# Moving head turns, feeds of merged sums and a wait for the last head into neighbouring matmul blocks of a two-block transformer kernel

## What is computed

```python
proj = x @ w_in                                   # first block
q_dsa, c_kv, q_idx, k_idx, w_idx, q_m, k_m, v_m, ga, gb = split(proj)
merged = sigmoid(ga + b0) * (o_a @ w_o_dsa) + sigmoid(gb + b1) * (o_b @ w_o_moba)
y = merged @ w_out
...
y = (silu(g) * u) @ w_ffn_out                     # g, u = split(x @ w_ffn_in)
...
merged2 = sum(sigmoid(gate[n]) * (branch[n] @ w_up_2[n]) for n in range(3))
x = x + merged2 @ w_out_2                         # second block
```

## Time and profile before

| | |
|---|---|
| median of 3 runs | 2307.86 us (2304.59 to 2309.53) |
| the profiled execution | 2309.78 us, span 2307.9 us |
| PE, busy share of the span | 98% |
| DVE, ACT, POOL, busy share | 57%, 45%, 7% |
| mean granted clock of PE | 0.992 of full |
| moved by DMA | 421 MB, 182 GB/s on average |

### The profile page before, as it was taken

How to read it: one execution, slowest core, us unless ns; L and a number is a source line. 1 busy time by engine, 2 the same in 40 slices (tenths; PEclk the granted TensorE clock), 3 DMA queues, 4 the chain that set the end, 5 groups by cost and what they waited for, 6 DMA issues and landing times.

```text
span 2307.9 us, 30089 instructions
## 1 busy us (share of the span) xinstructions
PE 2253.7 (98%) x10189; PEld 1855.2 (80%) x10189; DVE 1305.9 (57%) x1571; ACT 1044.2 (45%) x1243; POOL 168.3 (7%) x175
## 2 busy tenths in 40 slices
PE   9999999999999899999999999998999999999999
PEld 7777888888877678878887888786888788888887
DVE  5445655666657665445444444457655566645664
ACT  4333444555434444433444344344445444545643
POOL 1000000001204040000000000004000000200020
PEclk9999999999999999999999999999999999999999
DMA  7654554655855456566665666554556565665555
GB/s 216 221 163 147 174 162 153 191 163 180 275 192 163 148 182 190 177 191 192 192 189 180 186 183 201 177 186 137 178 172 199 180 188 177 213 180 180 174 182 164
DMA packets 216698, 421.10 MB, mean 182 GB/s; under 512 B 15240, under 2 KB 19888, under 8 KB 214704
## 3 DMA queue, kind: packets, MB, share of 16 engines
q1 hardware_dynamic: 213456, 402.31, 56.6%
q0 software_dynamic: 3168, 17.82, 2.3%
HBM read 417.97 MB, written 2.11 MB: 182 GB/s over the span
## 4 chain that ended last, share of the span: by engine, by line
PE 94%; DVE 3%; ACT 1%; DMA 1%; issue 1%; DVEq 0%; SPq 0%; ACTq 0%
PE b_ps L543 88%; PE b_ps L585 1%; PE b_ps L568 1%; PE b_ps L628 1%; DVE b_w_lo L1321 1%; DVE b_x_res L1479 1%; PE b_ps L698 1%; DMA b_stage<-in_w_up 1%; DVE b_x_res L1470 1%; PE b_ps L643 1%; PE b_ps L637 0%; PE b_ps L716 0%; PE b_ps L644 0%; ACT b_nat L986 0%; DMA b_gate_a<-in_x 0%
## 5 line engine op out<-in xcount | busy, mean ns | idle before, releaser
L1321 DVE TENSOR_TENSOR b_w_lo<-b_stage,b_w_hi 128x1024 fp32r<-128x1024 f32 (+1 forms) x762 | 931.5, 1242 | 605.1 <-ACT b_w_hi L959 599.1
L959 ACT ACTIVATE b_w_hi<-b_stage 128x1024 fp32r<-128x1024 f32 (+1 forms) x762 | 793.9, 1054 | 706.2 <-PE b_ps L543 674.0
L543 PE MATMUL b_ps<-b_w_hi,b_x_hi 128*128 128x512 f32 (+1 forms) x2368 | 943.6, 399 | 4.5 <-DVE b_x_lo L1362 3.0
L543 PE MATMUL b_ps<-b_w_hi,b_x_lo 128*128 128x512 f32 (+1 forms) x2368 | 923.8, 390 | 0.0
L543 PE MATMUL b_ps<-b_w_lo,b_x_hi 128*128 128x512 f32 (+1 forms) x2368 | 922.5, 390 | 0.0
L543 PEld LDWEIGHTS b_ps<-b_w_hi,b_x_hi 128*128 128x128 f32 x2368 | 447.2, 189 | 101.1 <-issue 6.4
L543 PEld LDWEIGHTS b_ps<-b_w_hi,b_x_lo 128*128 128x128 f32 x2368 | 446.4, 189 | 94.1
L543 PEld LDWEIGHTS b_ps<-b_w_lo,b_x_hi 128*128 128x128 f32 x2368 | 447.3, 189 | 87.9
L543 PE MATMUL b_ps<-b_w_hi,b_ff_h 128*128 128x512 f32 x352 | 138.9, 395 | 6.2 <-DVE b_ff_l L1362 6.2
L543 PE MATMUL b_ps<-b_w_hi,b_ff_l 128*128 128x512 f32 x352 | 138.3, 393 | 0.0
L543 PE MATMUL b_ps<-b_w_lo,b_ff_h 128*128 128x512 f32 x352 | 138.2, 393 | 0.0
(11 more groups left out here) (280 smaller groups left out, 1463.0 us busy)
## 6 DMA issues: line engine op xcount, KB each, us to landing
b_stage<-in_w_in SPq DMA_DIRECT2D x336, 512.0 KB, 4.0
b_stage<-in_w_ffn_in SPq DMA_DIRECT2D x176, 512.0 KB, 4.5
b_stage<-in_w_ffn_out SPq DMA_DIRECT2D x88, 512.0 KB, 4.2
b_stage<-in_w_out SPq DMA_DIRECT2D x64, 512.0 KB, 4.3
b_stage<-in_w_up SPq DMA_DIRECT2D x24, 512.0 KB, 4.3
b_stage<-in_w_o_dsa SPq DMA_DIRECT2D x16, 512.0 KB, 4.3
b_stage<-in_w_o_moba SPq DMA_DIRECT2D x16, 512.0 KB, 4.3
b_stage<-in_w_kv_mem SPq DMA_DIRECT2D x16, 512.0 KB, 3.9
```

What stands on the lines that cost most here:

```text
L543: ins = mm(ps[:, ACC + r, 0:n], x[:, kt + t, rows], w[:, slot, t, 0:n], start=first and t == 0 and k == 0, stop=last and t == GK - 1 and k ...
L959: act.activation(w_hi[:, slot, :, 0:n], stage[:, slot, :, 0:n], ACT.Copy)\
L1321: dve.tensor_tensor(w_lo[:, slot, :, 0:n], stage[:, slot, :, 0:n], w_hi[:, slot, :, 0:n].bitcast(F32), ALU.subtract).then_inc(sem("lo_done ...
```

## The change

1. **Turns.** The 8 turns of the q and k projections stand behind group 0 of the block that follows, on PE and on DVE (which copies the heads there). The turn of the index keys and the latent (`keys_and_latent`, 7 transposes) stands behind group 2. The loops over these blocks are written out.
2. **Last turn of each `ffn_in` part.** It stands behind group 0 of the first `ffn_out` block, and that block waits for it only ahead of the group that reads its result.
3. **Last head.** The wait for `o_free` stands ahead of the last group of an up-projection block.
4. **Feeds of merged sums.** Batches of the feed stand behind groups of the up-projection blocks 1 to 3, as `FED_UP_B` and `FED_UP_2` say (block: {group: batch}), and the rest in the first block of the output projection. ACT and DVE have their parts at the same places.
5. **Bias table.** POOL waits for the end of the first branch's up-projection and for each of the 8 loads before it posts the next.
6. **Start.** The first weights are posted ahead of `x`; `keep_warm` runs 18 and 3 transposes in place of 12 and 10; ACT and DVE split the first group ahead of the first batch; DVE reads out the first block ahead of its last split.

```diff
+FED_UP_B = ({}, {2: 0, 3: 1}, {2: 2, 3: 3}, {2: 4, 3: 5}, {2: 6, 3: 7})
+FED_UP_2 = ({}, {1: 0}, {0: 1, 1: 2}, {0: 3, 1: 4}, {0: 5, 2: 6, 3: 7})
...
             x_chunk(0, 0, NB // 2)
-            group(a["w_in"], 0, C_LAT, FIRST_W)
             x_chunk(0, NB // 2, NB)
             group(a["w_in"], GK * P, C_LAT, FIRST_W)
...
+                    pool.wait_ge(sem("tile_out1"), c.at("ups0") + 4)
...
+                            pool.wait_ge(sem("rel"), c.next("rel", 16))
...
-            keep_warm(12)
-            feed_weights(x_in, x_landed, n=FIRST_W, warm=lambda: keep_warm(10))
-            with c.loop(pe, "q_idx", 2):
-                weights()
-                turn(left)
...
-            with c.loop(pe, "q_dsa", 2):
-                weights()
-                turn(left)
-            with c.loop(pe, "qk_m", 4):
-                pe.wait_ge(sem("qi_staged"), c.next("qi_staged"))
...
-                weights(hook=index_head)
-                turn(left)
-            for b in range(2):
-                weights()
+            keep_warm(18)
+            feed_weights(x_in, x_landed, n=FIRST_W, warm=lambda: keep_warm(3))
+            def turn_first(then=None):
+                def hook(j):
+                    if j == 0:
+                        turn(left)
+                    if then:
+                        then(j)
+                return hook
+            def keys_and_latent(j):
+                if j != 2:
...
+                T(ps[:, TP, S:S + P], kidx2[:, 0, :], ident[:, :]).then_inc(sem("tp_done"), 1)
...
+            def index_head(j):
...
+                if n == 0:
+                    pe.wait_ge(sem("qi_staged"), c.next("qi_staged"))
...
+            weights()
+            weights(hook=turn_first())
+            weights(hook=turn_first(keys_and_latent))
+            weights(hook=turn_first())
+            for b in range(4):
+                weights(hook=turn_first(index_head))
+            weights(hook=turn_first())
+            weights()
...
-            pe.wait_ge(sem("o_free"), c.value("o_free"))
+            def last_head_at(group_):
+                def before(j):
+                    if j == group_:
+                        pe.wait_ge(sem("o_free"), c.value("o_free"))
...
-                weights(kts=8, hi=oh, lo=ol)
+                weights(kts=8, hi=oh, lo=ol, before=last_head_at(3))
...
-            pe.wait_ge(sem("o_free"), c.value("o_free"))
-            with c.loop(pe, "up_b", 4):
-                weights(kts=8, hi=oh, lo=ol)
...
-            feed_weights(gate_a, merged_by("summed1"))
+            def feed_one(src, t):
+                pe.wait_ge(sem("tp_free"), c.value("tp_free", 0 if t == 0 else 1))
+                feed_batch(src, t)
+            def merged_by(mark, n):
+                pe.wait_ge(sem("summed"), max(1, c.at(mark) - D // NB + n + 1))
+            def feed_when(src, mark, batches):
+                def hook(j):
+                    if j in batches:
+                        t = batches[j]
+                        merged_by(mark, t // 2)
+                        feed_one(src, t)
+                return hook
+            def fed_by(j):
+                if j == 0:
+                    pe.wait_ge(sem("tp_free"), c.value("tp_free"))
+                elif j >= 5:
+                    pe.wait_ge(sem("tp_free"), c.value("tp_free", 7 - j))
+            for b in range(4):
+                weights(kts=8, hi=oh, lo=ol, before=last_head_at(3),
+                        hook=feed_when(gate_a, "summed1", FED_UP_B[b]))
+            weights(before=fed_by, hook=feed_when(gate_a, "summed1", FED_UP_B[4]))
...
-                turn(left)
-                pe.wait_ge(sem("tp_free"), c.value("tp_free"))
+                def last_tile_at(j):
+                    if j == 2 * (nf - 1):
+                        pe.wait_ge(sem("tp_free"), c.value("tp_free"))
+                weights(kts=4 * nf, hi=ff_h, lo=ff_l, before=last_tile_at, hook=turn_last)
...
-                pe.wait_ge(sem("o_free"), c.value("o_free"))
-                with c.loop(pe, f"up2_{n}", 2):
-                    for b in range(2):
-                        weights(kts=4, hi=y_h, lo=y_l)
-            feed_weights(merged2, merged_by("summed_b2"))
+                if n < 2:
+                    with c.loop(pe, f"up2_{n}", 2):
+                        for b in range(2):
+                            weights(kts=4, hi=y_h, lo=y_l, before=last_head_at(1))
+                else:
+                    for b in range(4):
+                        weights(kts=4, hi=y_h, lo=y_l, before=last_head_at(1),
+                                hook=feed_when(merged2, "summed_b2", FED_UP_2[b]))
+            weights(before=fed_by, hook=feed_when(merged2, "summed_b2", FED_UP_2[4]))
...
+            split()
             for t in range(KT // 2):
                 lo_batch(x_hi[:, 2 * t:2 * t + 2, :], x_lo[:, 2 * t:2 * t + 2, :], t)
-                split()
+                if t > 0:
+                    split()
                 c.next("w_used")
-            for _ in range(AHEAD):
-                split()
+            split()
             for r in range(R):
                 tile_done(r)
...
                 c.next(f"tile_out{r}")
...
+            def heads_of(b):
+                dst, b = (qi_t, b) if b < 2 else (qd_t, b - 2) if b < 4 else (qkm_t, b - 4)
+                heads_in(lambda t: dst[:, b * 4 + 2 * t:b * 4 + 2 * t + 2, :])
+            for b in range(8):
+                def q_hook(j):
+                    if b > 0 and j == 0:
+                        heads_of(b - 1)
+                        if b == 2:
+                            c.mark("q_idx", "tp_free")
+                    if b == 0:
+                        small_norms(j)
+                    if b == 2 and j == 2:
+                        keys_and_latent()
+                    if b >= 4:
+                        if j == 0 and b == 4:
...
             c.mark("ups_b", "tile_out1")
-            with c.loop(dve, "up_b", 4) as i:
-                weights(kts=8)
...
+            def feed_when(batches):
+                def hook(j):
+                    if j in batches:
+                        t = batches[j]
+                        lo_batch(x_hi[:, 2 * t:2 * t + 2, :], x_lo[:, 2 * t:2 * t + 2, :], t)
+                return hook
+            for b in range(4):
+                weights(kts=8, hook=feed_when(FED_UP_B[b]))
+                gated_at(gate_b, gate_a, slice(b * NB, (b + 1) * NB), True)
             c.mark("merged", "tile_out1")
-            feed_weights(x_hi, x_lo)
+            weights(hook=feed_when(FED_UP_B[4]))
             c.mark("fed", "tp_free")
...
-                product_lo(nf - 1)
                 alpha = ALPHA if f0 == 0 else 1.0
                 stat = f0 == FFN_PARTS[-1][0]
```

More of the change, by code:

```diff
@@ new lines, in index_head @@
+            def index_head(j):
+                if j % 2:
+                    return
+                n = j // 2
+                half = slice((n % 2) * IDX_D, (n % 2 + 1) * IDX_D)
+                if n == 0:
+                    pe.wait_ge(sem("qi_staged"), c.next("qi_staged"))
+                pe.wait_ge(sem("idx_read"), c.value("idx_read"))
+                for t, (lo, hi) in enumerate(TILE_COLS):
+                    ins = mm(ps[:, AUX, lo:hi], qi_st[half, n // 2, t * P:(t + 1) * P],
+                             kidx_t[half, 0:hi - lo], start=True, stop=True)
+                ins.then_inc(sem("idx_done"), 1)
+                c.next("idx_read")
@@ L1063, in _ @@
             c.next("tp_done", 2)
-            with c.loop(act, "q_dsa", 2):
+            for b in range(2):
                 weights()
@@ L1197, in _ @@
                     hidden(hook=lambda j: product_hi(i) if j == 0 else None)
-                product_hi(nf - 1)
+                weights(kts=4 * nf, hook=lambda j: product_hi(nf - 1) if j == 0 else None)
+                skip_block()
                 if nf == 4:
-                    with c.loop(act, f"ffn_out{f0}", 4):
+                    with c.loop(act, f"ffn_out{f0}", 3):
                         weights(kts=4 * nf)
@@ L1203, in _ @@
                 else:
-                    with c.loop(act, f"ffn_out{f0}", 2):
-                        for b in range(2):
-                            weights(kts=4 * nf)
-                            skip_block()
+                    for b in range(3):
+                        weights(kts=4 * nf)
+                        skip_block()
             root(sd[:, 0:R])
@@ L1579, in _ @@
             dve.wait_ge(sem("ext"), 32)
-            for b in range(2):
-                weights(hook=small_norms if b == 0 else None)
-                skip_block()
-                heads_in(lambda t: qi_t[:, b * 4 + 2 * t:b * 4 + 2 * t + 2, :])
-            c.mark("q_idx", "tp_free")
-            dve.wait_ge(sem("tp_done"), c.next("tp_done"))
-            dve.tensor_copy(kidx_t[:, :], ps[:, TP, 0:S]).then_inc(sem("tp_free"), 1)
-            dve.wait_ge(sem("tp_done"), c.next("tp_done"))
```

(31 more changed lines are left out.)

144 lines of the change are left out of this document (73 added, 71 removed).

## The result

The changed kernel takes 2311.46 us (median of 20 runs, 2308.12 to 2312.53) and the kernel before, run beside it, 2306.59 us (20 runs, 2303.46 to 2309.53): a ratio of 1.0018, 95% interval 1.0011 to 1.0024. It is 4.9 us slower, where 7.5 us less were forecast. The predicted time was 2300, its range 2292 to 2307.

What follows compares the result with a forecast made beforehand. PE was taken to bound the kernel (94% of the chain that ended last). Gains of 29.1 us against losses of 21.6 made -7.5, from 2309.78 to 2302.3, less 1.9 for the profiled execution: 2300, range 2292 to 2307.

Steps and rivals of the forecast that it cites:

- the turns of q and k: Between q and k projection blocks: turns moved behind a group 0 cost 0.79 us each; gain 6.5 us, bounds 5 to 7.
- the last turns of `ffn_in`: End of the three `ffn_in` parts: waits at the turn go, gain 8.7 us, plus 3.2 for two half-clock stretches.
- the last head: Before the first up-projection: PE's 1.4 us wait goes, as its first three groups read finished heads; gain 1.4 us.
- the bias table: First branch's up-projection: the late weight load's 3.4 us wait and 1.6 us half-clock stretch go; gain 5.0, bounds 0 to 5.0.
- the six new stalls: Up-projection block boundaries: `gated` queues behind `lo_batch` on DVE, so PE waits 2.3 us at each of six; loss 13.8 us.
- the feeds: Feeds of `merged` and `merged2`: 16 batches placed behind groups cost 7.7 us in place of 5.3 and 4.9; gain 2.6.
- the clock behind the stalls: After the six new stalls: half clock follows 3 of 6; loss 4.8 us, bounds 0 to 9.6.
- Loads behind the merge: At `w_out`: POOL's two load bursts become one, about one group of weights is missing; loss 3 us, bounds 0 to 11.
- The share of the weights: During POOL's burst at `w_out`, the weights' queue was taken to move 0.06 to 0.09 MB/us, from the earlier trace.
- the start: Kernel start: fewer transposes let group 0 start 1.4 us earlier; gain 1.7 us, bounds loss 1.4 to gain 3.
- The weights starve behind the merge: Rival at `w_out`: PE stands 18 us for weights, giving 2317; milder form, 6 to 12 us, 2303 to 2309; chance 0.12.
- The bias table's rival: The table's loads still hold up weights, now in the projection behind: 5 us more, 2305; chance 0.08.

Runs made afterwards that it cites:

- late_mem: Changed kernel with `mem_nat` and the small tables behind it loaded after the second `w_out` block: 2308.46 us, ratio 1.0008 to the kernel before.
- early_x: Changed kernel with `x_res` loaded at the start of the second up-projection: 2300.02 us, ratio 0.9973 to the kernel before.
- quarters: Changed kernel with `x_res`, `vec_a`, `vec_b` and `mem_nat` each loaded in four transfers of 512 columns (2 KB rows): 2303.91 us, ratio 0.9978 to the kernel before.
- residual_first: Changed kernel with DVE reading out the first `w_out` block ahead of the split of group 195: 2306.80 us, ratio 1.0000 to the kernel before.
- bias_alone: Kernel before with only the bias table's part of the change: 2303.64 us, ratio 0.9986 to the kernel before.
- old_start: `gated_first` with the start of the kernel before: 2282.23 us, ratio 0.9891 to the kernel before.
- gated_early_x: `gated_first` with `x_res` loaded at the start of the second up-projection: 2278.53 us, ratio 0.9878 to the kernel before.
- old_feeds: Changed kernel with both feeds of merged sums as in the kernel before: 2282.72 us, ratio 0.9894 to the kernel before.
- gated_first: Changed kernel with DVE's read-out `gated` ahead of `lo_batch` behind a block's last group, in six places: 2283.69 us, ratio 0.9899 to the kernel before.

## Why the prediction was wrong

**What held.** On the timelines of the two executions: the turns of q and k -6.7 (forecast -6.5), the last turns of `ffn_in` with their two half-clock stretches -12.1 (-8.7 and -3.2), the last head -1.7 (-1.4), the bias table -5.3 (-5.0), the six new stalls 6 x 2.35 = +14.1 (+13.8), the feeds -2.9 (-2.6), the clock behind the stalls +4.6 (+4.8). The last is right in size, but by luck in this execution: 3 of 6 were taken, and it was all three of `merged2` and none of `merged`, where `late_mem`, `early_x`, `quarters` and `residual_first` lose 1.6 to 3.3 us too. The wins in their sum, 26.5 without the feeds, measured 23.9 by medians.

**The step that failed** is "Loads behind the merge": +3.0 taken, 11.4 measured (`early_x` against the changed kernel) and 11.9 on the timelines, past the upper of its bounds of 0 to 11. That the bursts run together and that weights of `w_out` are then missing was right, as were the two posts that it starts from (forecast: 3.5 and 13 us after group 0 of `w_out`; measured 3.5 and 13.7). But the step reckoned only when PE multiplies, and left out what DVE has to do first. Of the 8.9 us that were missing:
- *The lead*, 4.5 us on the timelines. I reckoned that weights land 3.7 groups ahead of need. PE's need is not what they are late for. DVE's list has the split of the group after next ahead of the read-out of a block, so at a block's boundary PE waits for weights two groups on. `residual_first` takes this away alone (4.7 us by medians).
- *The clock*, 1.7 us. Group 194, behind the wait, took 4.4 us instead of 2.72, at half clock. This was left out of the middle value.
- *The rest*, 2.7 us, is bytes: without the order and the clock the late weights still cost some 5.7 us where 3.0 were taken. No run sets apart why. The share of the weights is not the reason: I took 0.06 to 0.09 MB/us from the earlier trace rows, and 0.084 came (0.84 MB in 10 us).

**The share was right and its reason was not seen.** The window of the earlier trace rows holds two things. Loads of weights were posted from 593.61 us on, and up to 597.4 us no packet of theirs moved. From then on the two queues move packets one for one, already in the kernel before (from 598 to 606 us):

```profile
q0 software_dynamic: 343, 2.55, 76.4%
q1 hardware_dynamic: 340, 0.66, 23.6%
```

So it is in the kernel after (445 against 443) and in `quarters` (673 against 673). I worked out what turns of equal bytes would give, found that the trace spoke against it, and stopped there. The Trainium skill (DMA: Bandwidth & Descriptors, Queues, rings and completion order) has an engine switch between queues a packet at a time. The trace agrees, as far as the packets that the profile counts are the unit meant; that they are, no run shows.

**The rivals.** "The weights starve behind the merge" came true in its milder form (a wait of 10 us, within its 6 to 12), for which I had given 2303 to 2309; at 0.12 it was too unlikely. Its argument "in the trace the weights always got a share" did not hold for the first 3.4 us of the window that it names, and was about the wrong quantity: a share counts only against the groups that must land before the boundary. The bias table's rival fell with `bias_alone`.

**The offset.** My sum by timelines, 2302.3, comes to 2311.2 with 11.9 in place of 3.0. The other terms above take off another 1.1 in sum, the start adds 0.3, and places that the change does not touch differ by -1.0 between the two executions. That gives 2309.4; the profiled execution of after took 2309.3. The forecast took 1.9 us off for the profiled execution of before, which lay above the median of 3 runs (by 3.2 against 20 runs). After the change the profiled execution lay 2.1 below its median. Differences by medians and by timelines are up to 5 us apart (`early_x`: 11.4 and 6.8), and what is left of the error (12.4 us between -7.5 and +4.9, of which the starving is 8.4) is of that kind. Why single executions of one kernel differ by some 1.6 us and its multiples was not settled; the stretches of lower clock that come and go between executions, as in `late_mem`, have this size.

**The start** was forecast at a gain of 1.7. Group 0 started 0.44 us later, not 1.4 earlier; group 1 followed it 0.9 us sooner, and the earlier read-out gained 0.9, which is 1.4 at group 8 in these two executions. That is not shown to be a gain: with the same new start group 8 began at 30.1 to 31.7 us in different kernels, with the old one at 30.5 to 31.9, and by `old_start` it is worth nothing.

**The feeds.** The 2.9 us are 1.6 at `merged` and 1.2 at `merged2`, on the timelines and without stalls and clock. By medians `gated_early_x` is 4.2 us below `old_feeds`; on their timelines 1 us of this is a late group at the end of the old feed.

The two edits that undo the losses, the read-out ahead of the low part and `x_res` early, give 2278.5 us: 33 us less than the changed kernel and 29 less than before (ratio 0.9878, 0.9863 to 0.9893). So this kernel is faster than both of them.

## What to carry to other kernels

When work is put behind the last group of a block, look on every engine at what is queued behind it: here one subtraction of 0.69 us ahead of the read-out, itself waiting for ACT and PE, cost 2.35 us at each of six places, and swapping the two gave back 27.8 us, where the whole change had cost 4.9. When two loads of another queue move closer together, count how many groups must have landed before the in-order engine reaches the next read-out, not how many before PE multiplies. And count a queue's share of the DMA engines in packets: the queue with long rows takes the bandwidth, and shorter rows or an earlier load take it back.

## What the runs showed of the hardware

- Two queues that both moved data moved packets one for one: 343 to 340 in 8 us of the kernel before, 445 to 443 in 10 us of the kernel after with 7.5 and 1.9 KB each, and 673 to 673 in `quarters` with 3.4 and 1.9 KB. The bytes follow from that, 3.32 to 0.84 MB and 2.31 to 1.29 MB.
- The first packet of a load of weights that was posted behind POOL's burst moved late: 3.8 us after its post in the kernel before, 3.6 after, 3.7 in `gated_first`, and 2.5 in `quarters`, where POOL's packets are half as long. In between POOL's queue moved, and of the weights nothing but what had been posted ahead of the burst.
- A 0.5 MB load posted 0.9 us ahead of a burst of 4 MB landed after 3.8 us, and one posted 1.3 us behind it after 12.3 us in the same trace.
- The granted clock behind a stall depends on what PE does in it. In the kernel after, the clock was at 0.50, its lower level, for 3.4 us behind each of the three stalls of `merged2` in which PE stood for 2.1 us, which cost 1.5 us each; with transposes in the same stalls it stayed at 1.00, its upper level. Standing still alone does not decide it: over six traces the clock fell behind 17 of 18 such stalls of `merged2` and behind 7 of 18 of `merged`.
